# The recurrent mixer's sums of forget logs, with 64 tokens' high and low parts stacked in the rows

## The chip, the cores and the metric

The kernel runs on one core of a Trainium2 chip. Its time is the device time of one execution in microseconds (us). A core has a matrix engine (TensorE, PE in the rows), whose weight loads are listed apart (PEld), a vector engine (VectorE, DVE), an activation engine (ScalarE, ACT), GpSimd (POOL) and SyncE (SP), which issues the DMAs here. They run on their own and wait for one another by semaphores. Matrix products are written to PSUM (eight banks of 128 rows x 512 floats); everything else lives in SBUF.

## The reference, cut to what matters

Two models run one after the other over 512 tokens: two hybrid layers, then two layers of feed-forward, mixer, cross-attention and feed-forward. The change is in the recurrent half of the mixer of the second model, which runs twice, once per layer, with 4 heads of 128 channels:

```
log_f = logaddexp(log(lb), log1p(-lb) + log_sigmoid(z))
k = (1.0 - lb) * sigmoid(-z)
b = cumsum(log_f)                      # within a chunk of tokens
o_inter = (q * exp(b)) S
decay[t, s] = exp(b[t] - b[s]), s <= t
A[t, s] = sum_k q[t, k] k[s, k] decay[t, s, k]
o = o_inter + A v
S = exp(b_last) * S + sum_s (k_s * exp(b_last - b_s)) v_s
```

## The kernel before

The kernel does this in 4 tiles of 128 tokens. `b[t] - b[s]` is never formed for all pairs. A tile of 128 tokens is halved again and again: level 0 splits it into two halves of 64 tokens, level 1 into quarters, and so on down to level 6. On each level a query in a right half and a key in the left half beside it meet at the border between them, so the exponent is a sum of log_f from the border up to t, plus a sum from s up to the border. Eight such sums are wanted per token and channel (seven levels, and the plain running sum as number 7). They are all products of log_f with 0/1 tables: the table `level` has 8 x 128 columns, and a column (level n, token t) holds a 1 for each token s that belongs to the sum.

For precision log_f (`LF`, tokens in the rows, 4 tiles of 512 channels in the columns) is split into a rounded high part (`LFhi`) and a low part (`ul`, the tile `ul_a`), each fit for a fast matmul. `sums(h, c)` (L2401) then does head h and token tile c: for each of two PSUM banks (4 levels of 128 columns each) one matmul with the high part held in the array and one with the low part, 512 columns each: four matmuls for one (h, c), two banks each time. ACT turns both banks into `E` with one exp of 1024 columns (`exps`, L2252). With four banks for this, `sums` of tile c waits for the exp of tile c-2.

After that, per head: DVE multiplies the right halves of `E` by the queries (`weigh`: seven operations at L2318 and one of 512 columns at L2322), GpSimd multiplies the left halves by the keys (L2239, seven operations), TensorE multiplies the two per level (`scores`, L2426, in five units, the last one L2429), DVE keeps what each level's mask allows (`keep`, L2335, and L2340 for the last unit), and TensorE makes the outputs (L2454, L2456). The order is written out by hand. `scores(h)` puts `sums` of later heads between its units: for head 0, `sums(2, 0)` after unit 3; for head 1, `sums(2, 2)` after unit 0, `sums(2, 3)` after unit 1 and `sums(3, 0)` after unit 3; for head 2, `sums(3, 2)` and `sums(3, 3)` after units 0 and 1. After `scores(0)` and `scores(1)` comes `turn_keys` (L2398) and then `sums(2, 1)` or `sums(3, 1)`, ahead of the outputs. Unit 2 waits for DVE's `weigh` of levels 4 and 5, which stands in DVE's queue behind `keep` of unit 0 and the head before's `finish`. A unit also waits for `keep` of the unit before the last one. `keep` of the last unit must be done before the outputs. The eight `sums` of heads 0 and 1 come first, before any scores.

Just before this stage ACT does, in this order and with no other engine between: copies the table for the sums after a token (`after`, L2130), reads the four heads of Q out of PSUM (L2132), copies the table of levels (L2133), makes `Kp` with four exps (L2136), reads `Kf` (L2246), and starts on `E`. The states also use `after` with the two parts of log_f (`PoolAndStates.tensor`, L2184 and L2185).

## Time and profile before

| | us |
|---|---|
| median of 3 runs | 2926.18 (2925.79 to 2926.19) |
| the profiled execution's own time | 2925.35 |
| its span | 2923.6 |
| PE busy | 2892.8 (99%) |
| PEld busy | 2501.0 (86%) |
| DVE busy | 2029.5 (69%) |
| ACT busy | 1297.4 (44%) |
| POOL busy | 575.4 (20%) |
| TensorE's share of the chain that ended last | 89% |
| DVE's and ACT's share of it | 6% and 3% |

The line of TensorE's granted clock has its highest digit, 9, in each of the page's 40 slices. The matmuls of this stage overlap in the profile: a row of 512 columns lasts 0.39 us but the next one starts 0.23 us after it. What a matmul costs is therefore read from starts, not from durations, and "99% busy" doesn't mean that TensorE never waits. The stage stands twice in the span, at 1201 to 1285 us and at 2288 to 2373 us.

### The profile page before, as it was taken

How to read it: one execution, taken by the hardware profiler on the slowest of the kernel's cores; microseconds unless marked ns; L12 is line 12 of the kernel's file. 1: busy time of each engine (PE TensorE's matmuls, PEld its weight loads, DVE VectorE, ACT ScalarE, POOL GpSimd, SP SyncE). 2: the span in 40 equal slices, each digit the busy share in tenths (PEclk: the TensorE clock that was granted, in tenths of full speed). 3: DMA queues.
4: the chain of work that ended last, by engine and by line, in shares of the span. 5: the costliest groups of instructions: out<-in, count | busy, mean ns of one | idle time of the engine just before them, and what ended most of it. 6: DMA issues, size and time to landing. Idle time of an engine off the chain costs nothing.

```text
span 2923.6 us, 40420 instructions
## 1 busy us (share of the span) xinstructions
PE 2892.8 (99%) x16738; PEld 2501.0 (86%) x16738; DVE 2029.5 (69%) x2542; ACT 1297.4 (44%) x1619; POOL 575.4 (20%) x380
## 2 busy tenths in 40 slices
PE   8999999999999999999999999999999999999998
PEld 6786877868899988888889998899988888889997
DVE  5656556565788884575668887788874665678887
ACT  5545445354534335434543333443346434443332
POOL 0000000000344310200033441343400200034431
PEclk9999999999999999999999999999999999999999
DMA  4121221212233232113222222322332123222222
GB/s 162 44 87 51 101 87 44 89 61 89 99 119 106 101 114 105 35 64 134 91 87 101 101 102 101 108 101 92 111 110 101 43 73 130 80 93 102 101 102 73
DMA packets 41959, 270.10 MB, mean 92 GB/s; under 512 B 5776, under 2 KB 6032, under 8 KB 10672
## 3 DMA queue, kind: packets, MB, share of 16 engines
q1 hardware_dynamic: 41776, 267.52, 25.8%
q8 instruction: 132, 2.16, 0.3%
q14 instruction: 51, 0.42, 0.0%
HBM read 265.33 MB, written 2.10 MB: 91 GB/s over the span
## 4 chain that ended last, share of the span: by engine, by line
PE 89%; DVE 6%; ACT 3%; issue 1%; DVEq 1%; DMA 0%; POOL 0%; SPq 0%; ACTq 0%; POOLq 0%
PE PS L313 27%; PE PS L315 26%; PE PS L314 26%; PE PS L691 1%; PE PS L2426 1%; PE PS L1211 1%; DVE w_lo L287 1%; PE PS L1239 1%; ACT w_hi L279 1%; DVE XT L1724 1%; DVEq L1697 1%; PE PS L750 1%; PE PS L1052 0%; DVE ff_a L1711 0%; PE PS L2406 0%
## 5 line engine op out<-in xcount | busy, mean ns | idle before, releaser
L287 DVE TENSOR_TENSOR w_lo<-w_raw,w_hi 128x2048 fp32r<-128x2048 f32 x167 | 382.6, 2291 | 308.5 <-ACT w_hi L279 307.2
L279 ACT ACTIVATE w_hi<-w_raw 128x2048 fp32r<-128x2048 f32 x169 | 323.2, 1912 | 419.4 <-PE PS L315 419.2
L313 PE MATMUL PS<-uh_b,w_hi 128*128 128x256 f32 (+1 forms) x1096 | 358.9, 327 | 0.0
L315 PE MATMUL PS<-uh_b,w_lo 128*128 128x256 f32 (+1 forms) x1096 | 357.9, 327 | 0.0
L314 PE MATMUL PS<-ul_b,w_hi 128*128 128x256 f32 (+1 forms) x1096 | 357.7, 326 | 0.0
L209 ACT ACTIVATE w_hi<-w_raw 128x1536 fp32r<-128x1536 f32 x72 | 107.3, 1491 | 477.8 <-PE PS L315 477.8
L313 PE MATMUL PS<-uh_a,w_hi 128*128 128x512 f32 (+1 forms) x792 | 288.7, 364 | 1.1 <-DVE ul_a L639 0.7
L314 PE MATMUL PS<-ul_a,w_hi 128*128 128x512 f32 (+1 forms) x792 | 285.5, 360 | 0.0
L315 PE MATMUL PS<-uh_a,w_lo 128*128 128x512 f32 (+1 forms) x792 | 285.5, 360 | 0.0
L313 PE MATMUL PS<-ff_h_hi,w_hi 128*128 128x512 f32 x704 | 278.4, 395 | 5.0 <-DVE XT L1724 4.5
L314 PE MATMUL PS<-ff_h_lo,w_hi 128*128 128x512 f32 x704 | 274.5, 390 | 0.0
L315 PE MATMUL PS<-ff_h_hi,w_lo 128*128 128x512 f32 x704 | 274.4, 390 | 0.0
L313 PE MATMUL PS<-w_hi,uh_a 128*128 128x512 f32 x640 | 252.5, 395 | 7.4 <-DVE ul_a L373 7.4
L314 PE MATMUL PS<-w_lo,uh_a 128*128 128x512 f32 x640 | 250.0, 391 | 0.0
L315 PE MATMUL PS<-w_hi,ul_a 128*128 128x512 f32 x640 | 249.9, 390 | 0.0
L313 PE MATMUL PS<-TA_hi,w_hi 128*128 128x256 f32 x864 | 244.5, 283 | 0.0
L314 PE MATMUL PS<-TA_lo,w_hi 128*128 128x256 f32 x864 | 244.5, 283 | 0.0
L315 PE MATMUL PS<-TA_hi,w_lo 128*128 128x256 f32 x864 | 244.5, 283 | 0.0
L196 POOL TENSOR_TENSOR w_S<-w_raw 128x512 f32<-128x512 f32 x72 | 123.9, 1721 | 593.4 <-DMA w_raw<-in_weights 356.8
L1724 DVE SCALAR_TENSOR_TENSOR XT<-PS,XT 128x1024 f32<-128x1024 f32 x175 | 213.2, 1218 | 34.5 <-PE PS L315 34.1
L314 PEld LDWEIGHTS PS<-ul_b,w_hi 128*128 128x128 f32 x1096 | 208.4, 190 | 18.3
L313 PEld LDWEIGHTS PS<-uh_b,w_hi 128*128 128x128 f32 x1096 | 208.4, 190 | 18.1
(400 smaller groups left out, 6549.5 us busy)
## 6 DMA issues: line engine op xcount, KB each, us to landing
w_raw<-in_weights SPq DMA_DIRECT2D x241, 1024.0 KB, 4.8
XT<-in_xT SPq DMA_DIRECT2D x8, 256.0 KB, 6.1
mem_raw<-in_mem SPq DMA_DIRECT2D x2, 1024.0 KB, 5.4
out<-XT SPq DMA_DIRECT2D x8, 256.0 KB, 2.0
bands<-in_bands SPq DMA_DIRECT2D x2, 768.0 KB, 6.3
w_raw<-in_weights SPq DMA_DIRECT2D x4, 256.0 KB, 4.7
p_raw<-in_pT SPq DMA_DIRECT2D x2, 512.0 KB, 3.8
lb<-in_lb_logits SPq DMA_DIRECT2D x2, 512.0 KB, 5.7
```

What stands on the lines that cost most here:

```text
L196: pool.tensor_tensor(s3, a11, a21, ALU.add)
L209: act.activation(self.hi[g % 2][:, 0:1536], self.raw[g % 2][:, 0:1536], ACT.Copy).then_inc(self.hi_first_done.sem, 1)
L279: act.activation(self.hi[g % 2][:], self.raw[g % 2][:], ACT.Copy).then_inc(self.hi_done.sem, 1)
L287: dve.tensor_tensor(self.lo[g % 2][:], self.raw[g % 2][:], self.hi[g % 2][:], ALU.subtract).then_inc(self.lo_done.sem, 1)
L313: pe.matmul(out, sh, mh, start=first, stop=False, skip_group_check=onto)
L314: pe.matmul(out, sh, ml, start=False, stop=False, skip_group_check=onto)
L315: return pe.matmul(out, sl, mh, start=False, stop=last, skip_group_check=onto)
L691: i = pe.matmul(self.at[t], self.m.QT[0:HEAD + 2, h, t * P:(t + 1) * P], self.m.KT[0:HEAD + 2, h, 0:(t + 1) * P], start=True, stop=True)
L750: i = pe.matmul(self.at(odd, t), self.m.QP[rows, pair, t * P:(t + 1) * P], self.m.KP[rows, pair, 0:(t + 1) * P], start=True, stop=True, ti ...
L1211: i = pe.matmul(self.k.PS[odd * HEAD:(odd + 1) * HEAD, 7, j * P:SEQ], m.V[:, j, h * HEAD:(h + 1) * HEAD], m.PT[h % self.BUFFERS][:, PTOFF[ ...
L1239: i = pe.transpose(flat[:, a:a + P], self.S(h)[:, SOFF[t] + j * P:SOFF[t] + (j + 1) * P], self.k.ident)
L1724: i = dve.scalar_tensor_tensor(x, k.PS[:, b:b + 2, :], 0.5, x, ALU.mult, ALU.add)
```

## The change

A sum of one level over tokens in the left 64 of a tile only ever serves columns of those 64 tokens, and the same holds for the right 64, but for one: the running sum (number 7) of a right token also holds all 64 left ones. So the table is cut in two: 8 levels x 64 columns for the left tokens, and the same for the right ones, each a table of 64 rows, written twice over one another. The rows freed in the array take the low part: `early` holds the high part of the left 64 tokens in rows 0 to 63 and their low part in rows 64 to 127; `late` holds the low part of the right 64 tokens in rows 0 to 63 and their high part in rows 64 to 127. One matmul of 512 columns then sums high and low part at once. `sums(h, c)` is three matmuls: `late` with its table (512 columns), `early` with ones onto the 64 columns of the running sum, and `early` with its table (512 columns).

To fill the two stacked tiles, DVE writes the left tokens' low part in the projection stage; ACT writes the right tokens' high part in two operations behind the projection, and DVE their low part in two. The exp reads and writes the new column order.

```
+HALFP = P // 2
-    second = np.concatenate([ident, level.reshape(P, -1), after], 1)
+    levels_of = [np.tile(level[a:a + half, :, a:a + half].reshape(half, -1), (2, 1)) for a in (0, half)]
+    after_of = [np.tile(after[a:a + half], (2, 1)) for a in (0, half)]
+    second = np.concatenate([ident] + levels_of + after_of, 1)
...
     # MixerProjection.scalar
-        act.activation(m.LFhi[:, :, 0:DA], m.LF[:], ACT.Copy).then_inc(self.lf_hi.sem, 1)
+        act.activation(m.LFhi[0:HALFP, :, 0:DA], m.LF[0:HALFP], ACT.Copy).then_inc(self.lf_hi.sem, 1)
     # MixerProjection.vector
         w.split_lo(dve, g0 + 7)
+        dve.wait_ge(*self.lf_hi.at(1))
+        dve.tensor_tensor(m.LFhi[HALFP:P, :, 0:DA], m.LF[0:HALFP], m.LFhi[0:HALFP, :, 0:DA], ALU.subtract)
...
     # PoolAndStates.scalar
-        act.activation(uh[:, 6, 0:P], m.after, ACT.Copy).then_inc(self.tables_hi.sem, 1)
+        act.activation(uh[:, 6, 2 * P:2 * P + HALFP], k.ones[:].to_broadcast([P, HALFP]), ACT.Copy)
+        act.activation(uh[:, 6, 0:2 * P], m.after, ACT.Copy).then_inc(self.tables_hi.sem, 1)
+        for a in (0, 2):
+            act.activation(self.u[1][HALFP:P, a:a + 2, :], m.LF[HALFP:P, a:a + 2, :], ACT.Copy).then_inc(self.proj.lf_hi.sem, 1)
     # PoolAndStates.vector
-        dve.tensor_tensor(self.u[1][:, 0:NT, :], m.LF[:], m.LFhi[:, :, 0:DA], ALU.subtract).then_inc(self.lf_lo.sem, 1)
+        for a in (0, 2):
+            dve.wait_ge(*self.proj.lf_hi.at(2 + a // 2))
+            dve.tensor_tensor(self.u[1][0:HALFP, a:a + 2, :], m.LF[HALFP:P, a:a + 2, :], self.u[1][HALFP:P, a:a + 2, :],
+                              ALU.subtract).then_inc(self.lf_lo.sem, 1)
...
     # Recurrence.scalar
-               k.PS[:, b:b + 2, :].rearrange("p a (l t) -> p (a l) t", t=P), ACT.Exp).then_inc(self.exped.sem, 1)
+               k.PS[:, b:b + 2, :].rearrange("p a (l t) -> p a l t", t=HALFP), ACT.Exp).then_inc(self.exped.sem, 1)
...
     # Recurrence.tensor, sums(h, c)
-            for half in range(2):
-                bank = k.PS[:, 2 * (c % 2) + half, :]
-                pe.matmul(bank, self.states.lf_hi_of(c)[:, h * P:(h + 1) * P], uh[:, 4 + half, :], start=True, stop=False)
-                i = pe.matmul(bank, ul[:, c, h * P:(h + 1) * P], uh[:, 4 + half, :], start=False, stop=True)
-            i.then_inc(self.summed.sem, 1)
+            early, late = (part[:, h * P:(h + 1) * P] for part in self.states.parts(c))
+            first, second = k.PS[:, 2 * (c % 2), :], k.PS[:, 2 * (c % 2) + 1, :]
+            pe.matmul(second, late, uh[:, 5, :], start=True, stop=False)
+            pe.matmul(second[:, LEVELS * HALFP:], early, uh[:, 6, 2 * P:2 * P + HALFP], start=False, stop=True)
+            pe.matmul(first, early, uh[:, 4, :], start=True, stop=True).then_inc(self.summed.sem, 1)
```

The states' own sums keep their two matmuls, now with the two tables of `after_of`, and wait for DVE's two low parts one by one. The eight small matmuls of `decays` take their column of ones from `k.ones`.

On ACT, at the head of the stage before (the copy of `after`, Q, the level table, the table load for exp, `Kp`, `Kf`, the first head's `E`):

```order
L2130 ACTIVATE uh_a<-table_139 128x128
L2132 ACTIVATE Q_221<-PS 128x512 x4
L2133 ACTIVATE uh_a<-table_139 128x1024
L2136 ACT_TABLE_LOAD
L2136 ACTIVATE Kp<-PS 128x512 x4
L2246 ACTIVATE Kf_178<-PS 128x512
L2252 ACTIVATE E_173<-PS 128x8x128 x4
```

The same place now:

```order
L2136 ACTIVATE uh_a<-ones 128x64
L2137 ACTIVATE uh_a<-table_139 128x256
L2139 ACTIVATE ul_a<-LF 64x1024 x2
L2141 ACTIVATE Q_221<-PS 128x512 x4
L2142 ACTIVATE uh_a<-table_139 128x1024
L2145 ACT_TABLE_LOAD
L2145 ACTIVATE Kp<-PS 128x512 x4
L2257 ACTIVATE Kf_178<-PS 128x512
L2263 ACTIVATE E_173<-PS 128x2x8x64 x4
```

Three operations are new ahead of the reads of Q, the `after` copy is twice as wide, and nothing is gone.

On TensorE, head 1: unit 0 of the scores, `sums(2, 2)`, unit 1, `sums(2, 3)`, units 2 and 3, and the start of `sums(3, 0)`, before:

```order
L2426 MATMUL PS<-E_172 128x64 x8
L2406 MATMUL PS<-uh_a,LF_hi 128x512
L2407 MATMUL PS<-uh_a,ul_a 128x512
L2406 MATMUL PS<-uh_a,LF_hi 128x512
L2407 MATMUL PS<-uh_a,ul_a 128x512
L2426 MATMUL PS<-E_172 128x64 x8
L2406 MATMUL PS<-uh_a,LF_hi 128x512
L2407 MATMUL PS<-uh_a,ul_a 128x512
L2406 MATMUL PS<-uh_a,LF_hi 128x512
L2407 MATMUL PS<-uh_a,ul_a 128x512
L2426 MATMUL PS<-E_172 128x64 x12
```

The end of that stretch now, from unit 1 to the last unit:

```order
L2437 MATMUL PS<-E_172 128x64 x8
L2417 MATMUL PS<-uh_a,ul_a 128x512
L2418 MATMUL PS<-uh_a,LF_hi 128x64
L2419 MATMUL PS<-uh_a,LF_hi 128x512
L2437 MATMUL PS<-E_172 128x64 x12
L2417 MATMUL PS<-uh_a,ul_a 128x512
L2418 MATMUL PS<-uh_a,LF_hi 128x64
L2419 MATMUL PS<-uh_a,LF_hi 128x512
L2440 MATMUL PS<-Q_221,Kf_179 128x128 x4
```

Each group of four matmuls has become three, at the same places between the units.

## Rows read from the trace of the kernel before

**Rows 1.** The chain, 1200 to 1210 us: start us, us, engine, tile and line.
```profile
1200.98 0.31 ACT uh_a L2130
1201.29 1.95 ACT Q L2132 x4
1203.24 0.94 ACT uh_a L2133
...
1208.05 0.93 ACT E L2252
```
**Rows 2.** ACT's timeline of the first head (start, us), and an operation on 64 rows.
```profile
1207.90 1.98 ACT L2252 ACTIVATE E<-PS 128x1024 f32<-128x1024 f32 x2
...
1210.25 1.95 ACT L2252 ACTIVATE E<-PS 128x1024 f32<-128x1024 f32 x2 [0.37 <-PE PS L2407]
...
L894 ACT ACTIVATE KT<-PS 64x2048 f32<-64x2048 f32 x2 | 3.7, 1872 | 0.0
```
**Rows 3.** Waits of TensorE over the span: total us, times, longest.
```profile
PE PS L2406 <- ACT E L2252: 1.1, 4, 0.4
```
**Rows 4.** DVE's timeline, heads 0 to 2.
```profile
1212.30 5.77 DVE L2318 TENSOR_TENSOR E<-E,Q 128x256 f32<-128x256 f32 x7 [2.08 <-ACT E L2252]
...
1219.26 0.68 DVE L2162 COPY St<-PS 128x512 f32<-128x512 f32 x1
...
1225.62 1.25 DVE L2335 COPY_PREDICATED AT<-masks,PS 128x256 f32<-128x256 uint8 x2 [0.85 <-PE PS L2426]
...
1228.39 0.73 DVE L2340 COPY_PREDICATED AT<-masks,PS 128x512 f32<-128x512 uint8 x1 [0.62 <-PE PS L2429]
...
1237.55 0.43 DVE L2318 TENSOR_TENSOR E<-E,Q 128x256 f32<-128x256 f32 x1 [0.17 <-issue]
1237.89 0.69 DVE L2322 TENSOR_TENSOR E<-E,Q 128x512 f32<-128x512 f32 x1
1238.62 1.25 DVE L2335 COPY_PREDICATED AT<-masks,PS 128x256 f32<-128x256 uint8 x2
...
1241.39 0.75 DVE L2340 COPY_PREDICATED AT<-masks,PS 128x512 f32<-128x512 uint8 x1 [0.62 <-PE PS L2429]
...
1246.18 0.98 DVE L2335 COPY_PREDICATED AT<-masks,PS 128x256 f32<-128x256 uint8 x2 [0.28 <-PE PS L2426]
...
1250.73 0.43 DVE L2318 TENSOR_TENSOR E<-E,Q 128x256 f32<-128x256 f32 x1 [0.17 <-issue]
1251.07 1.22 DVE L2322 TENSOR_TENSOR E<-E,Q 128x512 f32<-128x512 f32 x1
```
**Rows 5.** TensorE's timeline, heads 0 and 1.
```profile
1220.04 6.44 PE L2426 MATMUL PS<-E 128*128 128x64 f32 x56
...
1227.30 1.05 PE L2429 MATMUL PS<-Q,Kf 128*128 128x128 f32 x8
...
1229.55 0.61 PE L2454 MATMUL PS<-V,AT 128*128 128x128 f32 x4
...
1232.82 0.47 PE L2406 MATMUL PS<-uh_a,LF_hi 128*128 128x512 f32 x1
...
1233.83 1.89 PE L2426 MATMUL PS<-E 128*128 128x64 f32 x16
...
1240.30 1.05 PE L2429 MATMUL PS<-Q,Kf 128*128 128x128 f32 x8
```
**Rows 6.** DVE's timeline in the projection.
```profile
1164.02 2.29 DVE L287 TENSOR_TENSOR w_lo<-w_raw,w_hi 128x2048 fp32r<-128x2048 f32 x1 [8.59 <-ACT w_hi L279]
```
**Rows 7.** GpSimd's timeline, keys of heads 2 and 3.
```profile
1237.91 5.83 POOL L2239 TENSOR_TENSOR E<-E,Kf 128x256 f32<-128x256 f32 x7 [11.43 <-ACT E L2252]
1250.97 5.58 POOL L2239 TENSOR_TENSOR E<-E,Kf 128x256 f32<-128x256 f32 x7 [7.24 <-ACT E L2252]
```
**Rows 8.** Clock near the end: matmuls (start, us), then window, PE, PEld, DVE, ACT, POOL, clock.
```profile
2910.14 1.95 PE L2801 MATMUL PS<-ones,square 128*128 128x1 f32 x16 [1.33 <-ACT square L364]
...
2912.00:2913.00 1.00, 1.00 (x9) 1.00 (x9) 0.00 (x0) 0.00 (x0) 0.00 (x0) 0.84 0.02 8
```

More of the change, by code:

```diff
@@ L2180, in tensor @@
         pe.wait_ge(*self.tables_hi.at(1))
-        pe.wait_ge(*self.lf_lo.at(1))
         for c in range(NT):
+            pe.wait_ge(*self.lf_lo.at(1 + c // 2))
             pe.wait_ge(*self.proj.qread.at(c + 1))
-            pe.matmul(k.PS[:, 4 + c, :], uh[:, 6, 0:P], self.lf_hi_of(c), start=True, stop=False)
-            pe.matmul(k.PS[:, 4 + c, :], uh[:, 6, 0:P], ul[:, c, :], start=False, stop=True).then_inc(self.suffix.sem, 1)
+            early, late = self.parts(c)
+            pe.matmul(k.PS[:, 4 + c, :], uh[:, 6, 0:P], early, start=True, stop=False)
+            pe.matmul(k.PS[:, 4 + c, :], uh[:, 6, P:2 * P], late, start=False, stop=True).then_inc(self.suffix.sem, 1)
     def decays(self, pe):
@@ L2191, in decays @@
                 d = (c - 1) * HH + h
-                i = pe.matmul(k.PS[:, 4, d:d + 1], m.LF[:, c, h * P:(h + 1) * P], m.level[:, LEVELS * P + P - 1:LEVELS * P + P],
-                              start=True, stop=True)
+                i = pe.matmul(k.PS[:, 4, d:d + 1], m.LF[:, c, h * P:(h + 1) * P], k.ones[:], start=True, stop=True)
         i.then_inc(self.dec.sem, 1)
@@ L2387, in tensor @@
     def tensor(self, pe):
-        k, m, right, (uh, ul) = self.k, self.m, self.right, self.u
+        k, m, right, uh = self.k, self.m, self.right, self.u[0]
         def turn_keys(h):
```

17 lines of the change are left out of this document (8 added, 9 removed).

## The prediction

> **What bounds the kernel now.** I read the page first, then the chain of waits through the first of the two recurrent stages, then the timelines of the engines there. The page says TensorE: 89% of the chain that ended last. That is an average, and the change lies in a stage of its own. The reader is to see three things there. First, for 7 us the chain runs on ACT alone, one operation behind the other, from the `after` copy to the first exp of `E` [rows 1]. Second, in the first head ACT's exps pace the sums: between the second and the third ACT idles 0.37 us for TensorE [rows 2], and TensorE waited for an exp four times in the span, two per stage, so both stages look alike [rows 3]. Third, from 1220 us on TensorE and DVE are close to a tie. DVE's idle time in head 1 (1233 to 1246 us) is 0.62 us before L2340 and 0.28 us before the next head's first unit, beside drains of 0.17 us [rows 4]. A faster TensorE therefore gets at most these 0.9 us there.
>
> **What the sums save.** Between the units of head 1 one `sums` takes 1233.83 - 1232.82 = 1.01 us of TensorE's queue [rows 5]: about 0.32 for the first matmul and 0.23 for each of three more. Now it is two of 512 columns and one of 64. For the one of 64 columns I take 0.11 us, the pace of the score matmuls, which have 64 columns too (56 records in 6.44 us, 0.115 each with the tail of the last) [rows 5]. It can't cost less than nothing nor more than one of 512 columns, 0.23. So 0.32 + 0.11 + 0.23 = 0.66 us, a saving of 0.35 us (bounds 0.23 to 0.46). For 32 `sums` that is 11.2 us of TensorE's time. What of it reaches the end is worked out place by place, for one stage.
>
> **The front, ACT.** Added ahead of Q: the ones (64 columns), the `after` copy grown from 128 to 256 columns, and two copies of 64 rows x 1024. An operation on 64 rows is no shorter: 64x2048 takes 1872 ns [rows 2]. The level table's 1024 columns take 0.94 us in the chain [rows 1], so the two copies are 1.88; by the same pace (0.87 ns per column) 128 more columns are 0.11, and 64 columns with their start about 0.16 (no less than 0.06, no more than the 0.31 of the `after` copy). Sum 2.15 us. Each microsecond of it is on the chain, since no other engine stands in it [rows 1]. The first exp starts at 1210.05 instead of 1207.90.
>
> TensorE now needs 0.35 us less for what ACT waits for in the middle of the head, so of the 0.37 us idle about 0.35 go, and with a start-up of its own 0.40. The four exps end 2.15 - 0.40 = 1.75 us later, and with them the start of DVE's `weigh` at 1212.30 [rows 4]. From there to the scores the chain is DVE's in both kernels: `weigh`, then the copy of the state that ends at 1219.94 [rows 4], against 1220.04 for the first score [rows 5]. TensorE, which ended its sums in the same moment, comes about 1 us early now, and that buys nothing. **Front: +1.75 us.**
>
> What covers the other new work: DVE's low part of the left tokens (as long as any pass over 2048 columns, 2.29 us) falls in the projection, where DVE sits idle 8.59 us between two weight blocks [rows 6]; if that cover went it would cost 2.3. DVE's pass over the low part of the right tokens is only cut in two; behind it in DVE's queue stand `mix` and `Kp`, which have to be done before the first exp at 1210, as they are by about 1210; Q's product ends near 1212, before 1214. The states' sums wait for Q, at 1203.8 to 1205.3, and are done before ACT's `Kp` at 1207.5. The exp in pieces of 64 columns I take as 0.94 us as before; bounds 0 and +0.1 each, eight of which stand on the chain.
>
> **Head 0.** `sums(2, 0)` stands before the last unit. That unit also waits for `keep` of unit 2, whose DVE operations end at 1226.87 [rows 4]; with 0.2 us for the drain and the semaphore, 1227.08 against 1227.30 [rows 5]: 0.22 us instead of 0.35. `sums(2, 1)` stands before the outputs. They come 2.25 us after the last unit's start (1227.30 to 1229.55) [rows 5], and DVE's L2340 is done 1.82 us after it (1229.12) [rows 4], so with 0.35 off, 1.90, both meet. **-0.57 us.**
>
> **Head 1.** `sums(2, 2)` and `sums(2, 3)` end earlier, but unit 2 waits for `weigh` of levels 4 and 5, which lies in DVE's unbroken queue: nothing. But the exps behind them are 0.7 to 0.8 us earlier too, and they release GpSimd, at about 1237.15 instead of 1237.91 [rows 7]. There DVE is about to weigh level 6 (1237.55, 0.43 us) and the plain sums (L2322, 0.69 us) [rows 4]. With GpSimd at work these are dear: the same L2322 one head later, under GpSimd's keys [rows 7], takes 1.22 us, and the seven of the first head take 5.77/7 = 0.82 each [rows 4]. So DVE loses 0.39 + 0.53 = 0.92 us ahead of unit 2, its end goes from 1239.87 to 1240.79, and the last unit starts at 1241.0 instead of 1240.30 [rows 5]: +0.70. `sums(3, 1)` gives 0.35 back. **+0.35 us.** Without the collision it would be 0.22 for the last unit and 0.28 for the next head's start, -0.50.
>
> The Trainium skill (SBUF — State Buffer, section "Who interferes with whom") says that a DVE instruction with two SBUF inputs contends with a GpSimd instruction that reads SBUF, and that one blocks until the other is done. The trace agrees: 1.22 against 0.69 us for the same form. By the rule the plain sums and level 6 block here too; without it the change would be cheaper by 1.2 us a stage.
>
> **Head 2.** `sums(3, 2)` and `sums(3, 3)` likewise buy nothing and bring GpSimd forward from 1250.97 [rows 7] to about 1250.2. L2322 is in collision already; now level 6 at 1250.73 [rows 4] is too: **+0.39 us**, or 0 without it. Head 3 has no sums and GpSimd has nothing left that is new; I count 0.
>
> **Sum.** One stage: 1.75 - 0.57 + 0.35 + 0.39 = +1.92 us; two: +3.84. The profiled execution had 2925.35, so 2929.2; its median stands 0.83 higher, which gives 2930.0.
>
> **The rivals.**
> 1. *No new collision.* GpSimd's earlier start falls between DVE's operations, or what DVE loses early it gets back in the next head's `weigh`, part of which lies under GpSimd's keys today. Then 1.75 - 0.57 - 0.50 = +0.68 a stage, +1.4 in all: 2927.5. For it: what GpSimd loses at one end it frees at the other. Against: L2322 at 1.22 us.
> 2. *TensorE bounds heads 0 to 2 after all.* Then the eight `sums` between the scores count in full: 1.75 - 8 x 0.35 = -1.05 a stage, 2924.1. Against it: DVE has 0.9 us of idle in head 1.
> 3. *The front is not paid.* If Q's reads were hidden behind TensorE, all 32 sums would count: -11.2, 2915.0. The chain speaks against it [rows 1].
> 4. *The clock falls*, slower by over 0.2%. In the new front TensorE waits longer: about 2 us ahead of `turn_keys`, 1.3 us between the sums, and then come 16 records of one column. At the end of this kernel such a stretch, 1.33 us of waiting and 24 records of one column, is followed by a granted clock of 0.84 and less, so the level of 1.2 GHz instead of 2.4 [rows 8]. At that level a 512-column matmul costs at least 0.2 us more. If it holds from the decays into the scores, over some 5 to 8 us of TensorE work, of which DVE's `weigh` covers part, it costs 2 to 4 us a stage: about 2936. It decides once the clock is still low when the scores begin. Against it: the page's clock line has a 9 in all 40 slices, these two stages with their gaps among them. The Trainium skill (TensorE: Matmul & The Clock Gate, "Why this matters for your kernels") lets the clock fall only over long idle gaps between bursts of matmuls. By that this rival would fall away and the forecast stand; the row at the end of the kernel, with a wait of 1.33 us, leaves it open.
>
> **How the numbers follow.** A measurement of this kernel can tell 0.2%, 5.9 us, from no change. Forecast (collision, 2930.0) 0.50; rival 1 0.26; rival 2 0.07; rival 3 0.03; rival 4 0.14. Unknown costs move the forecast: the 64-column matmul by 0.12 us at some four places on the chain, the exps by up to 0.1 at eight, the ones by 0.15, for two stages about -1 and +3. Range 2924.5 to 2934: it takes in rival 1, the edge of rival 2, and the forecast with its bounds; outside lie rival 3 and most of rival 4. Faster by over 0.2% is rival 3 and a part of what I have not seen: 0.05. Slower by over 0.2% is rival 4 and the forecast's upper edge: 0.16. The rest, 0.79, is no change.
>
> **What would show it.** The first exp of `E` 9.1 us after the stage's first ACT operation instead of 7.0; a `sums` at 0.66 us between units; L2322's counterpart in head 1 at about 1.2 us instead of 0.69; GpSimd's keys of head 2 starting 0.75 us earlier against DVE's first unit; the period from head 1's to head 2's first unit 13.5 us, where it was 13.1. I am wrong if that period falls to 12.6, if the front grows by less than 1.5 us, or if the clock's row in the front is below 1.00.

## The result, and the profile after

The changed kernel takes 2938.36 us, the median of 6 runs (2936.29 to 2942.05). The kernel before, on the same chip in the same minutes, takes 2926.06 us (6 runs, 2925.26 to 2926.29). The ratio is 1.0044, 95% interval 1.0033 to 1.0055: slower by more than the 0.2% that can be told from no change, above the predicted range of 2924.5 to 2934.0 and 8 us above its 2930.0. Its runs also lie further apart, 5.8 us against 1.0. TensorE's mean granted clock is 0.992 to 0.995 of full speed in these runs, and 0.998 in the runs of before. The profiled run took 2937.76 us with a span of 2935.9, so it lies 12.4 us above the profiled run of before (2925.35).

Both traces are read at the same instructions: the first ACT operation behind the projection, the first exp of `E`, DVE's first product, the first reduction of each head's output, the last low part of the stage (how late each comes against the kernel before is called its shift). Of the 12.4 us the first stage takes 4.2 and the second 6.2, where 1.92 each had been forecast; 0.4 come ahead of the first, 0.3 between them and 1.2 behind the second, where the low clock that ends the kernel before too sets in 1.3 us earlier against the work.

The first view to open is the clock by stretches. Columns: window, its length, busy time with count of PE, PEld, DVE, ACT and POOL, granted clock, DMA share, GB/s. In the kernel before the same windows (1200 to 1225 and 2295 to 2320 us) all have 1.00; one of them:

```profile
1210.00:1215.00 5.00, 5.00 (x42) 4.83 (x42) 2.92 (x5) 2.13 (x3) 2.66 (x3) 1.00 0.01 3
```

After, first stage, then second:

```profile
1205.00:1210.00 5.00, 2.81 (x13) 1.79 (x12) 3.81 (x7) 4.95 (x9) 0.99 (x2) 0.91 0.00 0
1210.00:1215.00 5.00, 4.75 (x23) 3.51 (x21) 3.19 (x3) 4.63 (x7) 0.00 (x0) 0.75 0.00 0
1215.00:1220.00 5.00, 5.00 (x31) 5.00 (x32) 4.53 (x6) 0.55 (x2) 4.48 (x6) 0.66 0.01 3
1220.00:1225.00 5.00, 4.39 (x29) 3.50 (x27) 4.80 (x11) 4.10 (x5) 1.94 (x2) 1.00 0.00 0
...
2300.00:2305.00 5.00, 4.04 (x13) 3.00 (x14) 4.10 (x4) 4.82 (x8) 0.78 (x2) 0.63 0.00 0
2305.00:2310.00 5.00, 5.00 (x23) 4.81 (x22) 2.47 (x4) 2.22 (x3) 2.43 (x3) 0.50 0.00 0
2310.00:2315.00 5.00, 5.00 (x25) 5.00 (x25) 4.59 (x6) 0.00 (x0) 3.98 (x5) 0.50 0.01 3
```

A clock of 0.50 is the level of 1.2 GHz. In the first stage it is low twice, 1209.1 to 1212.5 and 1215.9 to 1219.3 us; in the second once, 2301.3 to 2315.0, from the front to the end of the states. TensorE looks busy there (5.00 of 5 us) because each matmul lasts longer; the count tells it: 23 and 25 matmuls in 5 us. The page's line of forty slices, one digit each, can't show this: it has a 9 in every slice, as before.

The chain through the same place, against [rows 1] (start us, us, what):

```profile
1201.39 0.26 ACT uh_a L2136
1201.65 0.31 ACT uh_a L2137
...
1201.98 2.00 ACT ul_a L2139 x2
...
1204.00 2.07 ACT Q L2141 x4
...
1208.46 0.60 ACT Kp L2145
...
1209.12 1.11 PE PS L2409 x4
1210.23 0.43 PE PS L2417
...
1210.71 0.59 PE PS L2419
...
1212.40 1.03 ACT E L2263
```

Before, this chain was ACT's alone up to the first exp. Now TensorE is in it, with `turn_keys` (L2409) at 1.11 us where it had taken 0.66 and sums at the low clock. And TensorE's timeline (start, us, then the wait ahead in brackets):

```profile
1209.12 1.11 PE L2409 MATMUL PS<-ident,K 128*128 128x128 f32 x4 [2.19 <-ACT Kp L2145]
...
1215.85 4.55 PE L2218 MATMUL PS<-V,Kp 128*128 128x128 f32 x24
```

The states' 24 matmuls take 4.55 us; in the kernel before they take

```profile
1212.68 2.92 PE L2207 MATMUL PS<-V,Kp 128*128 128x128 f32 x24
```

In the second stage the decays (16 matmuls of one column) and the states both run at the low clock, and both are on the chain. The chain there, after:

```profile
2306.37 3.21 PE PS L2204 x16
2309.57 5.33 PE PS L2218 x24
```

and before (first stage):

```profile
1211.14 1.68 PE PS L2192 x16
1212.82 2.79 PE PS L2207 x24
```

8.54 us on the chain instead of 4.47: this alone is 4.1 us of that stage's 6.2.

The rows of the forecast's other terms, all at a clock of 1.00. First TensorE, a `sums` between two groups of scores in head 1:

```profile
1236.44 0.48 PE L2417 MATMUL PS<-uh_a,ul_a 128*128 128x512 f32 x1
1236.76 0.19 PE L2418 MATMUL PS<-uh_a,LF_hi 128*128 128x64 f32 x1
1236.79 0.47 PE L2419 MATMUL PS<-uh_a,LF_hi 128*128 128x512 f32 x1
1237.11 1.11 PE L2437 MATMUL PS<-E 128*128 128x64 f32 x9
```

It takes 1237.11 - 1236.44 = 0.67 us, forecast 0.66, where it was 1.01 [rows 5]. Then DVE and GpSimd in head 1:

```profile
1241.17 0.66 DVE L2329 TENSOR_TENSOR E<-E,Q 128x256 f32<-128x256 f32 x1 [0.17 <-issue]
1241.75 1.21 DVE L2333 TENSOR_TENSOR E<-E,Q 128x512 f32<-128x512 f32 x1
```
```profile
1240.82 5.71 POOL L2250 TENSOR_TENSOR E<-E,Kf 128x256 f32<-128x256 f32 x7 [10.26 <-ACT E L2263]
```

The products of level 6 and of the plain sums take 0.66 and 1.21 us, where they took 0.43 and 0.69 [rows 4]: the forecast collision with GpSimd's keys, which now start ahead of them and started behind before [rows 7]. What all this came to, as the shift against before, counted from the stage's first ACT operation:

```
shift, us            first exp  first product  outputs h0  outputs h1  stage end
forecast                +2.15       +1.75         +1.18       +1.53      +1.92
after, stage 1          +3.02       +2.76         +3.21       +3.41      +4.21
after, stage 2          +2.66       +3.01         +6.02       +6.24      +6.23
```

Most of the miss is made before the first score: it comes 3.67 us late in the first stage and 6.48 in the second. The clock is back at 1.00 by then. From the outputs of head 0 to the stage's end the two stages add 1.0 and 0.2 us, where 0.74 was forecast. The collision shows in head 2 too: its product of level 6 took 0.43 us before [rows 4] and takes 0.91 in the first stage and 0.59 in the second:

```profile
1254.87 0.91 DVE L2329 TENSOR_TENSOR E<-E,Q 128x256 f32<-128x256 f32 x1 [0.17 <-issue]
2349.13 0.59 DVE L2329 TENSOR_TENSOR E<-E,Q 128x256 f32<-128x256 f32 x1 [0.17 <-issue]
```

### The profile page after: what moved, and what is told of

Same layout as the page of the kernel before. It is cut to its first block, busy times and chain, and to the rows that moved or that the text cites. A ratio compares the mean times of both kernels' runs of the same rounds, so it can differ in the third digit from the quotient of the medians.

```text
span 2935.9 us, 40370 instructions
## 1 busy us (share of the span) xinstructions
PE 2895.3 (99%) x16706; PEld 2502.7 (85%) x16706; DVE 2033.7 (69%) x2546; ACT 1302.2 (44%) x1625; POOL 575.3 (20%) x380
## 4 chain that ended last, share of the span: by engine, by line
PE 88%; DVE 6%; ACT 3%; issue 1%; DVEq 1%; POOL 0%; DMA 0%; SPq 0%; ACTq 0%; POOLq 0%
PE PS L317 27%; PE PS L319 26%; PE PS L318 26%; PE PS L695 1%; PE PS L1215 1%; DVE w_lo L291 1%; PE PS L1243 1%; PE PS L2437 1%; DVE XT L1728 1%; ACT w_hi L283 1%; DVEq L1701 1%; PE PS L754 0%; PE PS L1056 0%; DVE ff_a L1715 0%; ACT SP L801 0%
```

## The experiments

Theory A: the stage's full clock hung on TensorE's work. The change took 47% of the columns of each `sums` (2048 to 1088) and lengthened the front's waits, and the granted clock falls to 1.2 GHz somewhere in the stage. Rival B: the added work in the front and the collision are dearer than forecast, and the low clock is a side show. Rival C: only the longer front waits let the clock fall, and the columns don't matter. Shifts are counted as in the table above, against the kernel before. The expectations below letter their rivals anew; where the text says "above", it means these three.

### 1. Idle matmuls in the front's waits

```
+    def fill(self, pe, bank, n):
+        for _ in range(n):
+            pe.matmul(k.PS[:, bank, :], uh[:, 6, 0:P], self.m.LFhi[:, 0, 0:DA], start=True, stop=True)
 ahead of turn_keys(0):       + self.states.fill(pe, 0, 9)
 ahead of sums(0, 2), (0, 3): + self.states.fill(pe, 5, 4), fill(pe, 5, 1)
```

> The changed kernel with 14 idle matmuls of 512 columns (their result is never read) put into TensorE's three waits of the first head: 9 ahead of turn_keys, 4 ahead of sums(0, 2), 1 ahead of sums(0, 3). Theory A (the clock): TensorE's longer waits at the head of the stage let its clock fall to 1.2 GHz, which costs 2.3 us in the first stage and 4.3 in the second beyond the 1.9 a stage that was forecast. Then the granted clock stays at 1.00 in both stages, the sixteen one-column records take 1.8 us and the states' 24 records 2.9, and the time is 2929.5 to 2931.5. Rival B (the front's operations and GpSimd's collisions alone cost what was measured, the clock only happens beside them): 2936.5 to 2939, as the changed kernel.

Measured: 2936.44 us, 5 runs from 2932.73 to 2946.64; ratio 1.0034 (1.0020 to 1.0049). In the profiled run, the slowest of them, the front keeps a clock of 1.00 and the states take 2.92 us again: first exp +2.56, first product +2.21. But then the clock falls in the scores, which it had not done in the profile after:

```profile
1220.00:1225.00 5.00, 4.07 (x19) 3.38 (x19) 4.76 (x11) 4.95 (x5) 3.06 (x5) 0.80 0.01 2
1225.00:1230.00 5.00, 5.00 (x25) 5.00 (x25) 1.40 (x4) 0.00 (x0) 3.38 (x5) 0.50 0.00 0
1230.00:1235.00 5.00, 5.00 (x25) 4.90 (x24) 1.96 (x4) 0.00 (x0) 0.00 (x0) 0.50 0.00 0
```
```profile
1222.62 11.66 PE L2444 MATMUL PS<-E 128*128 128x64 f32 x55 [0.52 <-issue]
```

55 score matmuls in 11.66 us, where 56 took 6.44 [rows 5]; that stage cost 11.1 us. The expected 2929.5 to 2931.5, with the clock held through both stages, was missed; by its median alone the run can't be told from the changed kernel. Filling the waits of the front keeps the clock in the front of this profile, and nothing more: rival C above can't be all. Work added to TensorE's waits cost nothing there: the first exp is no later than in experiment 3.

### 2. The same, with GpSimd's keys held back

```
             pool.wait_ge(*self.exped.at(NT * (h + 1)))
+            if h >= 2:
+                pool.wait_ge(*self.weighed.at(self.UNITS * h))
```

> As e1_fill, and GpSimd starts the keys of heads 2 and 3 only once DVE has weighed all levels of the head before. Theory A: DVE's L2333 there is back at 0.69 us and its level 6 at 0.43, the period from head 1's first unit to head 2's falls from 13.3 to 12.6 to 12.9 us and that of head 2 by 0.5 to 1 us; 1.5 to 3 us below e1_fill. Rival C (GpSimd's work is only moved, and hits the next head's weigh): within 0.5 us of e1_fill.

Measured: 2934.74 us, 5 runs from 2931.26 to 2941.99, ratio 1.0036 (1.0023 to 1.0049). Too far apart to tell the hold by the time. By the profile the outputs of head 1 follow those of head 0 in 0.23 us less than before, where the unheld kernels take 0.2 more. Experiments 10 and 11 ask it again.

### 3. The front alone

The kernel before with the four new ACT operations, whose results nothing uses:

```
+        act.activation(uh[:, 6, 2 * P:2 * P + 64], k.ones[:].to_broadcast([P, 64]), ACT.Copy)
+        act.activation(uh[:, 7, 0:P], m.after, ACT.Copy)
+        for a in (0, 2):
+            act.activation(uh[64:P, a:a + 2, :], m.LF[64:P, a:a + 2, :], ACT.Copy)
```

> The kernel before, with the four new operations of ACT alone (64 columns of ones, a second table copy of 128 columns, two copies of 64 rows x 1024), written where nothing reads them, and the old four-matmul sums. Theory A: the first exp of E comes 2.1 to 2.3 us later in each stage, all of it reaches the end: 2930.3 with the clock at 1.00, and up to 2936 where the 2.2 us of waiting ahead of turn_keys lets the clock fall. Rival D (ACT's work is hidden at the head of the stage): 2926.

Measured: 2933.36 us, 8 runs from 2931.18 to 2935.81, ratio 1.0026 (1.0015 to 1.0036). ACT's timeline:

```profile
1201.20 0.26 ACT L2130 ACTIVATE uh_a<-ones 128x64 fp32r<-128x64 f32 x1 [8.96 <-PE PS L315]
...
1201.88 2.00 ACT L2134 ACTIVATE uh_a<-LF 64x1024 fp32r<-64x1024 f32 x2
1203.89 2.07 ACT L2136 ACTIVATE Q<-PS 128x512 f32<-128x512 f32 x4
...
1210.75 1.99 ACT L2256 ACTIVATE E<-PS 128x1024 f32<-128x1024 f32 x2
```
```profile
1209.00 0.66 PE L2402 MATMUL PS<-ident,K 128*128 128x128 f32 x4 [2.25 <-ACT Kp L2140]
```

The first exp comes 9.55 us after the first ACT operation, 6.92 before: +2.63. In the first stage, at a clock of 1.00 throughout, every later mark of the table has 2.61 to 2.65 as well. So the front's work reaches the end in full, as forecast, and is 0.48 larger than forecast: the two copies take 2.01, not 1.88, the ones and the `after` table's second half 0.46, not 0.27 (0.37 in the changed kernel, where they are one operation less), and the four reads of `Q` behind them 2.09 from start to start, where they took 1.91. The same wait of TensorE as in the changed kernel, 2.25 us, let the clock fall in one stage (2299.8 to 2303.2, that stage +4.0) and not in the other.

### 4. The sums alone

The kernel before with three matmuls per `sums` from its own operands; the level sums lack a part:

```
-            for half in range(2): ... (four matmuls of 512 columns)
+            pe.matmul(second, late, uh[:, 5, :], start=True, stop=False)
+            pe.matmul(second[:, 448:], early, uh[:, 6, 0:64], start=False, stop=True)
+            pe.matmul(first, early, uh[:, 4, :], start=True, stop=True).then_inc(self.summed.sem, 1)
```

> The kernel before, with the sums as three matmuls (512, 64 and 512 columns) of the old operands, so that each level sum is incomplete, and nothing else. By the forecast's terms a stage gets -0.40 in the first head, -0.57, +0.35 and +0.39, so nearly nothing: 2925 to 2926. Rival E (TensorE bounds these heads, and each of the 32 sums gives its 0.35 us): 2915 to 2918.

Measured: 2930.26 us, 10 runs from 2926.73 to 2936.09, ratio 1.0016 (1.0007 to 1.0026), clock 0.994 to 0.997. Nothing is added here and 11 us of TensorE's work are gone, yet no run is below the median of the before runs beside it (2925.88), and the runs lie 9.4 us apart. Even in the fastest, which is the profiled one, the states run at the low clock:

```profile
1212.28 4.55 PE L2207 MATMUL PS<-V,Kp 128*128 128x128 f32 x24
```

Its second stage shows the savings without the clock: first product -0.36, outputs of head 0 -0.77. So head 0 gives 0.41 there. (Later in that stage, in head 2, the clock is low once more, 2339.5 to 2342.9.) This is the cleanest sign against rival B above: nothing is dearer, and the clock falls. Against rival C above it says that no longer front is needed. TensorE's wait between the sums of the front does grow, from 0.36 to 1.07 us, but only because the columns are gone while ACT's exps keep their pace:

```profile
1208.97 0.50 PE L2406 MATMUL PS<-uh_a,ul_a 128*128 128x512 f32 x1 [1.07 <-ACT E L2252]
```

### 5. Useless matmuls in every sums

The changed kernel with 896 columns added to each `sums`:

```
+            pe.matmul(first, early, uh[:, 4, :], start=True, stop=True)
+            pe.matmul(first[:, 0:384], early, uh[:, 4, 0:384], start=True, stop=True)
             pe.matmul(first, early, uh[:, 4, :], start=True, stop=True).then_inc(self.summed.sem, 1)
```

> The changed kernel, with two useless repeats of the last matmul (512 and 384 columns, same product into the same bank, before the one that is used) in every sums: each sums has 1984 columns on TensorE instead of 1088, about what it had before the change (2048), and takes some 1.05 us instead of 0.66. Nothing else changes. Theory A (the changed kernel is slow because TensorE, with fewer columns in the stage, is granted the lower clock in it): the added work makes the kernel faster. What is left is the front alone, so it should be where the kernel with the front alone is, 2931 to 2934, with no stretch of low clock in the scores, against 2938.4. Rival B (the clock fell for the longer waits in the front, and the columns of the sums don't matter): the clock falls as before, the added 0.4 us per sums comes on top where TensorE is the bound: 2938 or more. Rival C (the spread comes from elsewhere): the same 2936 to 2942.

Measured: 2933.81 us, 10 runs from 2931.89 to 2935.72, ratio 1.0025 (1.0016 to 1.0035), clock 0.996 to 0.998. Some 13 us of useless TensorE work make the changed kernel 4.5 us faster (4.3 when each is taken against the kernel before beside it; the two intervals still touch, 1.0033 to 1.0055 and 1.0016 to 1.0035): each of the ten runs is below the fastest run of the changed kernel, and each clock above its highest, 0.995. It comes out where the front alone does, as theory A said. This run's own rivals B (2938 or more) and C (2936 to 2942) fall. In the first stage the clock still falls in the front, 1209.3 to 1212.7 us, behind the wait ahead of `turn_keys`, and nowhere else before the kernel's end. The repeats do more than hold the clock. They make ACT's exps, and with them GpSimd's keys, later: level 6 of head 2 is back at 0.43 us, and from the outputs of head 1 to the stage's end this kernel takes 0.5 us less than the changed one in each stage, at a clock of 1.00 in both. But they cost more than that earlier: in the second stage, where the clock held, the first product comes at +2.67 (+2.20 in experiment 1), and from there to the outputs of head 0 it takes 0.20 us longer than before, where experiment 4 took 0.41 less. So the gain as a whole is the clock's.

### 6. The same, but not in the sums that something waits for

```
+            if h < 2 or c >= 2:   (around the two repeats)
```

> As the kernel with the repeats in every sums, but without them in sums(2, 0), sums(2, 1), sums(3, 0) and sums(3, 1), the ones behind which something waits at once. Theory A: if 28 of 32 repeats hold the clock as well, the savings of heads 0 and 1 come back, 0.4 to 0.6 us in head 0 and 0.2 to 0.35 in head 1, for two stages 1.2 to 1.9 us below the kernel with all repeats: 2929.5 to 2932. If the clock hangs on those last ones, it falls again in heads 0 to 2: above 2933. Rival B: the same as the changed kernel, 2936 to 2942.

Measured: 2932.87 us, 10 runs from 2932.13 to 2933.82, ratio 1.0023 (1.0013 to 1.0033). That lies between what theory A expected of a held clock (2932 at most) and of a fallen one (2933). The profile speaks for it: counted from the first product, the outputs of head 0 come 0.5 us earlier than with all repeats and those of head 1 0.6, and the clock falls only in the front, in both stages.

### 7. The exp's table loaded early

```
         w.split_hi(act, g0 + 10)
+        act.activation(m.dec[:, 0:1], k.ones[:], ACT.Exp)
```

> The kernel before, with one exp of a single column by ACT at the end of its work on the projection, its result overwritten later by the real one. In the profile of before ACT spends 1.28 us on a table load ahead of the first exp of the stage, in the middle of the chain that runs on ACT alone. Theory: each microsecond of that chain reaches the end (the front alone cost 2.6 and all of it came out), so moving the load into ACT's idle time ahead of the stage gives 1.28 us per stage, 2.5 in all: 2923.4, if no other table's load comes in its place. Rival: behind the exp stand copies that any table serves; if a copy loads another table, it is loaded twice: 2926 to 2928. Rival: ACT isn't idle at that place, and the load only moves along the path: 2925.9.

Measured: 2925.80 us, 10 runs, against 2925.81; ratio 0.9998 (0.9989 to 1.0008). The load does move, and 0.2 us of its 1.28 are won in each stage:

```profile
1192.60 1.28 ACT L2044 ACT_TABLE_LOAD   x1
...
1205.52 2.07 ACT L2137 ACTIVATE Kp<-PS 128x512 f32<-128x512 f32 x4 [0.77 <-PE PS L2186]
```

My theory was wrong. ACT's stretch in [rows 1] is unbroken, but the load in it covered a wait: without it ACT waits 0.77 us for the states' sums, and another 0.3 is lost between `Kf` and the first exp, which now waits for TensorE's `sums`. A chain without gaps does not say that everything in it can be taken away at a gain.

### 8 and 9. GpSimd makes the copies, with the repeats and without

```
-        for a in (0, 2):                                       (ACT)
-            act.activation(self.u[1][HALFP:P, a:a + 2, :], ...)
+        for a in (0, 2):                                       (GpSimd)
+            pool.tensor_copy(self.u[1][HALFP:P, a:a + 2, :], m.LF[HALFP:P, a:a + 2, :])
```

> The kernel with the repeats in every sums, but the two copies of 64 rows x 1024 (the high part of the right tokens' late rows) are made by GpSimd instead of ACT, beside ACT's after copy. Theory: ACT's front is 2.02 us shorter, and GpSimd's two copies and DVE's subtraction behind them are done by the time the states' sums want them: 2 x 2.0 below the kernel with all repeats, so about 2928. Rival: GpSimd's copies take over 2 us each and DVE's mix and Kp queue behind them, so that the first exp waits for Kp by DVE or TensorE: no gain, or slower.

> The kernel with GpSimd's two copies in place of ACT's and with the repeats (2928.66 us) once more, but without the repeats: 0.4 us less on TensorE in each of 32 sums, the front the same. Theory A (it is the columns that hold the clock): taking the useless work away makes the kernel slower, by a lower clock somewhere in each stage: 2931 to 2936, and the single runs lie further apart than the 3.7 us of the one with repeats. Rival B (the clock fell in the changed kernel for the longer front; here the front is 1.5 us shorter): the clock holds, heads 0 to 2 give back up to 0.5 us a stage, and it comes out at 2927.5 to 2928.5.

With repeats 2928.66 us, 10 runs from 2926.83 to 2930.49, clock 0.998 in each, ratio 1.0009 (1.0000 to 1.0019). Without them 2930.07, 10 runs from 2927.30 to 2939.91, clock 0.993 to 0.998, ratio 1.0015 (1.0006 to 1.0025). The medians don't tell the two apart, the spread does: 3.7 us against 12.6. The two kernels ran on different chips; experiments 9 and 12 on the same one, and there the clock is 0.993 to 0.998 without repeats and 0.998 in all ten runs with them (the twelfth has the early table and the hold besides). The ninth's median lies between what its theory A (from 2931) and its rival B (up to 2928.5) had expected. In its profile the front is shorter (first product +0.33, with repeats +1.20), and it is the clock that takes it back: it is low three times, for 3.4 us each. Rival B of the ninth, that a shorter front is enough to hold the clock, falls. The eighth comes out near its theory (about 2928). The first exp still comes 1.14 us late with the repeats, since DVE's two subtractions behind GpSimd's copies take 3.17 us (2.03 for the first, beside GpSimd's second copy, 1.22 for the other) and `mix` follows them:

```profile
1202.02 3.17 DVE L2156 TENSOR_TENSOR ul_a<-LF,ul_a 64x1024 fp32r<-64x1024 f32 x2 [7.68 <-POOL ul_a L2150]
1205.21 2.48 DVE L2160 TENSOR_TENSOR mix<-PS,pscale 128x512 f32<-128x512 f32 x4
```
```profile
1207.75 0.50 PE L2422 MATMUL PS<-uh_a,ul_a 128*128 128x512 f32 x1 [0.70 <-DVE mix L2160]
```

### 10 and 11. The collision, without and with the hold

The changed kernel with repeats under `if h < 2 or (h == 3 and c >= 2)`, and the same with GpSimd's wait of experiment 2.

> The changed kernel with the repeats in the sums of the early heads and in sums(3, 2) and sums(3, 3), but none in sums(2, 0) to sums(2, 3), sums(3, 0) and sums(3, 1). So in head 1 the exps come early again. Theory (collision): GpSimd's keys of head 2 start 0.7 us earlier than in the kernel with all repeats, DVE's product of level 6 takes 0.66 instead of 0.43 us and that of the plain sums 1.21 instead of 0.69, and from the outputs of head 0 to those of head 1 it takes 0.2 to 0.4 us longer than in the kernel with 28 repeats. 2933 to 2934.5 if the clock holds as there. Rival: the two products are as short as with repeats there, and the exps' earlier end costs nothing: the same 2932.9.

> The one before, with GpSimd's keys of heads 2 and 3 held back until DVE's last product of the head before is done (one wait more on GpSimd). Theory (collision): level 6 and the plain sums of head 1 take 0.43 and 0.69 us, 0.75 us less on DVE ahead of unit 2, of which the path gets 0.3 to 0.5; the same in head 2, where the kernel before pays 1.22 us too. For two stages 1.2 to 2 us less than without the wait: 2931 to 2932.5. Rival: what is gained there is lost in the next head's first products, which GpSimd's keys now run into: the same as without the wait.

Measured: 2932.85 (2930.77 to 2935.42) and 2932.57 us (2930.74 to 2935.60), 10 runs each, ratios 1.0024 (1.0014 to 1.0033) and 1.0021 (1.0012 to 1.0030): no difference in time that can be told, which is what the rivals of both had said (2932.9, and the same as without the wait). The profiles do tell the two apart. DVE in head 1 without the hold, and GpSimd:

```profile
1240.93 0.66 DVE L2329 TENSOR_TENSOR E<-E,Q 128x256 f32<-128x256 f32 x1 [0.17 <-issue]
1241.51 1.21 DVE L2333 TENSOR_TENSOR E<-E,Q 128x512 f32<-128x512 f32 x1
```
```profile
1240.59 5.72 POOL L2250 TENSOR_TENSOR E<-E,Kf 128x256 f32<-128x256 f32 x7 [10.26 <-ACT E L2263]
```

and with it:

```profile
1242.12 0.43 DVE L2331 TENSOR_TENSOR E<-E,Q 128x256 f32<-128x256 f32 x1 [0.17 <-issue]
1242.46 0.69 DVE L2335 TENSOR_TENSOR E<-E,Q 128x512 f32<-128x512 f32 x1
```
```profile
1243.32 5.48 POOL L2252 TENSOR_TENSOR E<-E,Kf 128x256 f32<-128x256 f32 x7 [11.81 <-DVE E L2335]
```

From the outputs of head 0 to those of head 1 the first takes 0.20 us longer than before, in both stages, the second 0.23 shorter, and with repeats there too (experiment 6) it is 0.05 shorter. So the collision is real. It costs the path 0.25 us in head 1 against experiment 6 and 0.43 against the hold; DVE loses 0.75 and has the rest in hand. Up to the last unit of head 2 the hold is worth 0.7 and 0.4 us in the two stages, counted from the outputs of head 0; of that 0.1 to 0.3 are given back in head 3, as the rival said, and 0.6 and 0.1 are left at the stage's end.

### 12 and 15. All that helped

Both kernels have GpSimd's copies, the early table and the hold; the twelfth repeats as in experiment 6, the fifteenth only in the four sums of head 1 and in sums(3, 2) and sums(3, 3).

> All that has helped, put together: GpSimd's copies in place of ACT's, the exp's table loaded ahead of the stage, the repeats in 28 of 32 sums, GpSimd's keys of heads 2 and 3 held back. From the kernel with GpSimd's copies and all repeats, 2928.66, the table load gives 0.2 a stage, the savings of heads 0 and 1 0.3, the hold 0 to 0.5: 2926.7 to 2927.7 if the clock holds, so still not below the kernel before (2925.8). Rival: with the hold worth what the case before it says in heads 2 and 3 both, 2925 to 2926. Rival: the clock falls again, 2930 and more.

> GpSimd's copies in place of ACT's, the exp's table loaded ahead of the stage, GpSimd's keys of heads 2 and 3 held back, and the repeats only in the four sums of head 1 and in sums(3, 2) and sums(3, 3). Theory: without the repeats of head 0 DVE's first product comes 0.3 instead of 1.2 us later than before, as in the kernel with GpSimd's copies and no repeats: 1.8 us below 2928.36, so 2926.5 if the clock holds. Rival: it falls somewhere in the stages as without any repeats: 2928 to 2932, runs far apart.

Measured: 2928.36 us (10 runs, 2927.02 to 2929.28; ratio 1.0006, 0.9997 to 1.0016) and 2929.37 us (10 runs, 2926.71 to 2935.09; ratio 1.0009, 1.0000 to 1.0019). In the first stage of the fifteenth, at a full clock, the change at last costs nothing: -0.04 at its end. In the second stage the clock is low from 2298.0 to 2308.2 us and it costs 4.12: this is the fifteenth's rival, and its expected 2926.5 was missed. In the twelfth the clock is 0.998 in every run and the stages cost 0.81 and 0.51; its median is above all that had been expected of a held clock (2926.7 to 2927.7). None of the versions beats the kernel before.

### 13 and 14. The clock held in both places

The idle matmuls of experiment 1 and the repeats of experiment 10 (13), or of experiment 15 (14), in the changed kernel.

> The changed kernel with both: the idle matmuls in the front's waits (as in the first experiment) and the repeats in the sums except sums(2, 0) to sums(2, 3), sums(3, 0) and sums(3, 1). Theory A (front waits and missing columns are the two places of the low clock, and nothing else is wrong): the clock holds through both stages, the first exp comes 2.6 us later, DVE's first product 2.2, head 1's first unit 0.3 to 0.5 less than that, and with the collision a stage costs 1.9 to 2.2: 2925.9 + 4.1 = 2930 to 2930.5. Rival B (a second cause of the miss, that the repeats only hide in part): still 2932.5 to 2933.5. Rival C: the idle matmuls are too much for the power of the chip and the clock falls elsewhere, as it did later in the profile of the first experiment: 2933 and more, runs far apart.

> The changed kernel with the idle matmuls in the front's waits and the repeats only in the four sums of head 1 and in sums(3, 2) and sums(3, 3). Theory A: if the clock holds, the first exp comes 2.6 us later than before, DVE's first product 2.2, head 1's first unit 1.9, head 2's 2.1, so a stage costs 1.6 to 2.3 us: 2925.9 + 3.9 = 2929.5 to 2930.5, what the prediction named. Rival B: the repeats of head 0 are what holds the clock in the scores, and without them it falls there as in the first experiment: 2932 and more, runs far apart. Rival C: a second cause: clock held and still 2932 to 2933.

Measured: 13, 2932.88 us, 10 runs from 2931.23 to 2934.01, ratio 1.0025 (1.0015 to 1.0035), clock 0.998 in all ten; 14, 2932.12 us, 10 runs from 2930.79 to 2934.85, ratio 1.0019 (1.0010 to 1.0029), clock 0.998 in nine of ten. The thirteenth's front, the same windows as after:

```profile
1205.00:1210.00 5.00, 4.87 (x24) 3.72 (x24) 3.84 (x7) 4.95 (x8) 1.00 (x2) 1.00 0.00 0
1210.00:1215.00 5.00, 5.00 (x31) 4.39 (x30) 2.43 (x2) 3.98 (x5) 0.00 (x0) 1.00 0.01 3
1215.00:1220.00 5.00, 5.00 (x41) 4.86 (x42) 4.74 (x7) 0.94 (x3) 4.70 (x6) 1.00 0.00 0
```

The clock holds through both stages, as theory A had it of the two places. Its time, 2930 to 2930.5, was missed by 2.4 us. By time the thirteenth looks like its rival B, but not by its profile: there the repeats of head 0 stand in the path of the exps, and the first product comes 3.31 us late in both stages instead of 2.2. The fourteenth leaves them out and has 2.20 and 2.21; its first stage, at a full clock, ends at +2.51, its second has a short low stretch (2305.9 to 2309.3) and ends at +3.19. Its median, 5.3 us above that of the before runs beside it (2926.82), is more than the forecast's 3.8. In the profile part of that is the low stretch, part lies outside the stages (1.2 us between the two); the cause of that part is open.

## Why the prediction was wrong

**The front, ACT: forecast +2.15 for the first exp, measured +2.55** for the changed kernel's own operations at a held clock (experiments 1, 13 and 14; +2.63 in experiment 3, which has one operation more). The mechanism held, each operation on the chain and all of it at the end. The size of its parts was low: two copies 2.02, not 1.88, the ones and the `after` table 0.37, not 0.27, and the reads behind them 0.18 longer.

**ACT's idle time between the exps: forecast -0.40, measured -0.35** in experiments 1, 4 and 14. Together the front is worth +2.2 instead of +1.75.

**Head 0: forecast -0.57.** In the profile after, from the first score to the outputs it takes 1233.07 - 1224.12 = 8.95 us, where it was 1229.55 - 1220.04 = 9.51 [rows 5]: -0.56. In experiment 4 it is -0.41 from the first product on.

**Head 1: forecast +0.35, measured +0.20** in both stages of experiment 10 and +0.21 in both of the profile after, with the collision as told (0.66 and 1.21 us). **Head 2: forecast +0.39,** and it is in the changed kernel itself, at a clock of 1.00, that it can be read: +0.80 in the first stage and -0.01 in the second, from the outputs of head 1 to the stage's end, the mean as forecast. Why the two stages differ is open. Experiment 10 can't stand for this term (+0.30 and -0.51): it has repeats in `sums(3, 2)` and `sums(3, 3)`, and level 6 of head 2 takes 0.43 us there, so the collision is missing.

At a held clock these make 2.2 - 0.41 + 0.20 + 0.80 = 2.8 us for the first stage and 2.2 - 0.41 + 0.20 - 0.01 = 2.0 for the second, 4.8 in all, where the forecast had 3.84. So the work comes to 1 us more than forecast, nearly all of it the front; this alone would have ended near 2931, inside the range. That is put together from several kernels; no single run showed 2930 or 2931, and experiment 14 with its 2932.12 stays above.

**The step that failed is the one left out of the sum: that the clock stays.** The stages cost 10.4 us instead of 4.8 in the profiled run, so 5.6 us of the 12.4 are the lower clock in them. The first score tells the same directly: with the clock held up to it (experiment 1) it comes 2.19 us late, in the profile after 3.67 and 6.48, so 1.5 and 4.3 us. With that the chain moved as well: the forecast had DVE's from the first product to the scores, and at the low clock it is TensorE's, through the decays and the states.

I had it as rival 4 with the right sign, at 0.14, a price of 2 to 4 us a stage (about 2936) and nearly the right place ("from the decays into the scores"). It was to decide once the clock is still low when the scores begin; in the profile after it is back before them, and decides all the same. The sign that I was wrong by was named too, a clock below 1.00 in the front, and it came: 0.91 and 0.75. Two things in it were wrong. I looked for the cause in the longer front alone, and experiment 4 shows the fall without that: taking the columns from the sums is enough. Experiment 4 computes with incomplete sums, but experiment 9, whose values are right and whose TensorE has no wait over 0.9 us up to the scores, shows it too. And I let the page's clock line, 40 digits of 73 us each, speak against it, though the low stretches are 3.4 to 13.7 us long and take less than a tenth from the mean of such a slice. By the Trainium skill (TensorE: Matmul & The Clock Gate, "Why this matters for your kernels") the rival would have fallen away; the measurement decides otherwise. The same page of the Trainium skill has another section, "A second HAM failure mode: psum-queue depth-cycling", where short idle times between groups of matmuls make the clock swing. I did not weigh it, and the runs here are nearer to it: waits of at most 2.3 us, and a clock that falls in one stage and not in the other of the same run (experiments 3, 5, 10 and 11).

The scale of what is lost can be read off: 24 matmuls of the states 4.55 us instead of 2.92, 55 of the scores 11.66 instead of some 6.3. What it costs hangs on the place. Where it falls into the front and the states, part is hidden behind ACT's exps and DVE's `weigh` (after, first stage: 6.8 us at the low level cost 1.5; second stage: 13.7 us cost 4.3). Where it reaches the scores, more of it counts: in experiment 1's first stage the outputs of head 0 come 8.08 us late, not some 1.8. That the place and length differ from run to run would explain the spread; only the profiled run of each kernel shows its places.

Counted over the profiles, two stages each: in 8 of the 12 stages with a wait of 2.2 us ahead of `turn_keys` (after, experiments 3, 5, 6, 10 and 11) the clock falls just behind that wait, in none of the 8 with idle matmuls in it (1, 2, 13, 14). In the stages without that wait it holds in all four of the kernel before and experiment 7 and in all four with the repeats (8 and 12), falls somewhere in all four without the columns (4 and 9), and in one of the two of experiment 15, which has the repeats in few of the sums.

**What stays open.** Which activity of TensorE exactly holds the clock isn't settled; these runs show only that the columns of the sums and the length of the waits both bear on it, and that it differs from run to run. About 1.9 us of the 12.4 lie outside the stages; 1.2 of them go with the earlier low clock at the end of the kernel. That part need not come from the change: from the second stage's end to the kernel's it took 556.5 us in the profile before, 557.7 after, and 557.9 in experiment 7, which leaves the stage nearly alone. The rest I can't place.

## What to carry to other kernels

A kernel whose TensorE works in short bursts between other engines can sit at the edge of the full clock. Before taking matmuls out of such a stage, look at the granted clock by windows of a few microseconds, there and at every other place with like waits, and give "the clock falls" the price of the stage's TensorE work at half speed. Afterwards, a wider spread of the runs together with a mean clock lower by a few thousandths is its mark, and useless matmuls put back into the stage are the test, read by the clock and not by the time alone: here they made the kernel faster and also pushed GpSimd's keys out of DVE's way.

And a chain that runs on one engine without a gap may still be a tie with another: take 1.28 us out and you may get 0.2.

## What the hardware showed that I had not expected

- Removing 11 us of TensorE's work and adding nothing made the kernel before 4.4 us slower in the median (experiment 4), and adding some 13 us to the changed kernel made it 4.5 us faster (experiment 5).
- The same program, same chip: 2927.30 to 2939.91 us in ten runs, with mean clocks of 0.998 to 0.993 (experiment 9). Nine idle matmuls of 512 columns in a wait of 2.2 us cost nothing, and in none of eight such stages did the clock fall just behind it.
- Four `Q` reads by ACT from PSUM took 2.07 us behind the new copies and 2.04 before, but 2.09 and 1.91 from the first's start to the next operation: what a group takes beside its record matters at this scale.
- Two casts of 64 rows x 1024 take GpSimd 2.02 us, much as ACT's 2.00. DVE's subtraction of 64 x 1024 takes 1.2 us alone (2.36 for two, experiment 5). In experiment 8 the first takes 2.03 us, with GpSimd's second cast beside it, and the second, with GpSimd done, 1.22 (3.17 for both).
